# A chunked two-way RWKV scan on one core: X and Y in one product by tokens, the removal terms on the opposite half of the partitions, the state summed over 128 partitions, and the solver's transfers on GpSimd's queue

## What is computed

```python
def _rwkv_step(S, inp):
    r, w, kk, kka, kt, v = inp
    sk = jnp.einsum('bhij,bhj->bhi', S, kk)
    S = S * w[:, :, None, :] - sk[..., None] * kka[:, :, None, :] + v[..., None] * kt[:, :, None, :]
    return S, jnp.einsum('bhij,bhj->bhi', S, r)
```

## Time and profile before

| | us |
|---|---|
| three runs: lowest, median, highest | 3841.0, 3841.06, 3845.65 |
| profiled execution | 3850.02 |
| its span, first to last instruction | 3848.3 |
| PE busy / DVE / ACT / GpSimd, of the span | 3417.3 / 1747.0 / 1178.4 / 552.4 |
| mean granted TensorE clock | 0.942 of 2.4 GHz |

### The profile page before, as it was taken

The page is one execution under the profiler, slowest core; times in us unless marked ns, Lnnn a source line. Parts: engine busy times, 40 slices in busy tenths (PEclk is TensorE's granted clock), DMA queues, the critical chain, the costliest instruction groups (busy, mean ns, idle before and its releaser), DMA issues.

```text
span 3848.3 us, 65362 instructions
## 1 busy us (share of the span) xinstructions
PE 3417.3 (89%) x28861; PEld 2311.7 (60%) x28861; DVE 1747.0 (45%) x2909; ACT 1178.4 (31%) x2057; POOL 552.4 (14%) x754
## 2 busy tenths in 40 slices
PE   6999989999999898745776899898989999989998
PEld 5777776343343766545664443236757888756887
DVE  4324641121222654963356222126855546855454
ACT  3225722111111565921112111003253234334233
POOL 2220120000000210048513000001102210101210
PEclk8999998999999998867888899999999999989999
DMA  6531147989886352987533999993203313212322
GB/s 246 184 107 52 61 167 266 375 313 370 317 313 262 124 182 98 313 223 183 145 102 133 344 415 420 419 420 133 88 22 118 113 62 107 70 54 99 101 86 77
DMA packets 314859, 739.32 MB, mean 192 GB/s; under 512 B 68248, under 2 KB 148896, under 8 KB 265424
## 3 DMA queue, kind: packets, MB, share of 16 engines
q1 hardware_dynamic: 302480, 697.18, 49.7%
q0 software_dynamic: 12096, 37.96, 3.1%
HBM read 673.19 MB, written 61.89 MB: 191 GB/s over the span
## 4 chain that ended last, share of the span: by engine, by line
PE 70%; DVE 10%; DMA 8%; ACT 5%; issue 2%; SPq 2%; POOL 0%; DVEq 0%; POOLq 0%; ACTq 0%
PE ps L62 66%; DMA raw<-in_moe_w_dram 6%; PE ps L66 4%; SPq L120 2%; DVE mx L75 1%; DVE mx L102 1%; DVE mrn L99 1%; DVE b L75 1%; DVE cr L75 1%; DMA Tb<-ot 1%; DVE o L75 1%; DVE o L81 0%; ACT cr L72 0%; DMA c<-in_w_ple_gate_dram 0%; ACT lw L72 0%
## 5 line engine op out<-in xcount | busy, mean ns | idle before, releaser
L62 PE MATMUL ps<-raw,xinT 128*64 128x512 f32 (+1 forms) x4096 | 591.6, 492 | 32.8 <-DMA raw<-in_moe_w_dram 23.6
L62 PEld LDWEIGHTS ps<-raw,xinT 128*64 128x64 f32 (+1 forms) x4096 | 196.0, 123 | 401.4 <-issue 288.1
L62 PE MATMUL ps<-wp,hp 128*128 128x512 f32 x1024 | 314.1, 393 | 8.6 <-ACT wp L72 8.6
L62 PE MATMUL ps<-cr,oTr 128*128 128x512 f32 (+2 forms) x1024 | 255.6, 382 | 3.5 <-ACT oTr L72 3.1
L75 DVE TENSOR_TENSOR mx<-mx,ps 128x512 f32<-128x512 f32 (+1 forms) x196 | 127.3, 663 | 234.6 <-PE ps L62 133.3
L62 PEld LDWEIGHTS ps<-wp,hp 128*128 128x128 f32 x1024 | 193.8, 190 | 49.0 <-issue 8.8
L62 PEld LDWEIGHTS ps<-cr,oTr 128*128 128x128 f32 x1024 | 187.6, 188 | 38.9 <-ACT oTr L72 3.6
L62 PE MATMUL ps<-wp,hTr 128*128 128x512 f32 x512 | 194.4, 389 | 0.0
L62 PE MATMUL ps<-raw,hidT 128*64 128x512 f32 x768 | 177.9, 602 | 3.2 <-DMA raw<-in_moe_w_dram 3.2
L62 PE MATMUL ps<-ar,naxh 128*128 128x512 f32 x576 | 147.4, 406 | 19.0 <-DVE ar L75 8.8
L75 DVE TENSOR_TENSOR wp<-c,wp 128x1536 fp32r<-128x1536 f32 x32 | 60.6, 1894 | 180.7 <-ACT wp L72 180.7
(11 more groups left out here) (535 smaller groups left out, 6332.4 us busy)
## 6 DMA issues: line engine op xcount, KB each, us to landing
raw<-in_moe_w_dram SPq DMA_DIRECT2D x384, 1024.0 KB, 7.7
c<-in_w_in_dram SPq DMA_DIRECT2D x28, 2048.0 KB, 9.3
mx<-in_ada_w_dram SPq DMA_DIRECT2D x14, 2048.0 KB, 8.0
raw<-in_ada_w_dram SPq DMA_DIRECT2D x8, 2048.0 KB, 13.5
a<-in_na_w_qkv_dram SPq DMA_DIRECT2D x6, 2048.0 KB, 7.9
c<-in_w_branch_dram SPq DMA_DIRECT2D x16, 512.0 KB, 5.9
c<-in_w_out_dram SPq DMA_DIRECT2D x4, 2048.0 KB, 10.8
c<-in_w_ple_gate_dram SPq DMA_DIRECT2D x4, 2048.0 KB, 7.9
```

What stands on the lines that cost most here:

```text
L62: return self.e.matmul(out, lhsT, rhs, start=start, stop=stop, skip_group_check=True) if self.e is not None else self
```

## The change

- Layout of the features: far and the lent place for b and k hold, per head pair, 256 columns: r or b of chunk 0, a or k of chunk 0, a or k of chunk 1, r or b of chunk 1. So pair(c) is 128 neighbouring columns with both kinds of one chunk. load fills them in six transfers per direction (r and b in halves).
- gram: one product of 128 loaded by 128 moving columns takes the place of two of 64 by 128.
- x1 and x2 load the 128 columns of pair(c): one product gives X on one half of the partitions and the first two terms of Y, by tokens, on the other. X and U of chunk c now stand on half(1 - c). x1 and y run in two turns (one half of the heads' banks each), with a wait of PE for itself between them. The x banks are held until y has been added (y: G with U), and DVE reads Y from them after each half step.
- V and U stand in one tile VU, V on the chunk's half and U on the opposite one, and tm holds b and k likewise. So s is one product over 128 partitions that sums V's and U's part; v is gone. One bank holds both directions; DVE adds it in one operation and multiplies by the decay in two.
- load_m issues twelve transfers a round (V comes with it), load_t four. V as a whole comes no more at the start; its four latent blocks come in rows_in(2).
- The order of work in a round is new (below). x1(r, 1) stands before s, level(r + 1, 0), x1(r + 1, 0) and level(r + 1, 1) behind y.
- const, with the fence for all stores of the features, stands before the solver's first 31 rows; squares 0, 1 and 2 are read together; emm is made in two operations. GpSimd itself stores T after its squares and reads the square after next. Its product space spr is now acc's sixth block, where square 0 lies, so square 1 waits for DVE's row 30.
- Banks gives out the bank that has been unused longest, and a released one goes to the end.
- Reader takes the mean from acc in SBUF; the transposes for it are gone.

```diff
-        while self.next % 8 in self.held.values():
-            self.next += 1
-        b = self.next % 8
-        self.next += 1
+        b = next(x for x in self.queue if x not in self.held.values())
+        self.last(b)
...
+    def last(self, b):
+        self.queue.remove(b)
+        self.queue.append(b)
...
-        del self.held[key]
+        self.last(self.held.pop(key))
...
+            e.wait_ge(*P.pool.at('row', 185))
...
+            e.wait_ge(*P.dve.at('y', self.last(c), 1))
+            e.tensor_reduce(m, hv(y), AX, ADD).then_inc(*P.dve.inc())
...
+            e.tensor_tensor(hv(y), hv(y), b16(m), SUB).then_inc(*P.dve.inc())
...
+    const()
     some(31)
-    const()
...
         recur(r, 0, 'x2')
-        recur(r, 0, 'y1')
-        recur(r, 0, 'y2')
+        if more:
+            gram(r + 1, 0)
         one(r)
         recur(r, 0, 'u')
-        recur(r, 0, 'v')
-        if more:
-            gram(r + 1, 0)
-            gram(r + 1, 1)
+        recur(r, 1, 'x1')
         some(4 if r else 8)
         recur(r, 0, 's')
+        recur(r, 0, 'y')
         one(r)
-        recur(r, 0, 'y3')
-        recur(r, 1, 'x1')
         if more:
-            gram(r + 1, 2)
-            gram(r + 1, 3)
-            blocks(r + 1)
+            gram(r + 1, 1)
         some(3 if r else 8)
         one(r)
         recur(r, 1, 'x2')
-        recur(r, 1, 'y2')
         if more:
-            level(r + 1, 0)
+            gram(r + 1, 2)
+            blocks(r + 1)
         one(r)
         some(3 if r else 7)
         recur(r, 1, 'u')
-        recur(r, 1, 'v')
         if more:
-            level(r + 1, 1)
+            gram(r + 1, 3)
         recur(r, 1, 's')
-        recur(r, 1, 'y3')
+        recur(r, 1, 'y')
         some(3)
         one(r)
         if more:
+            level(r + 1, 0)
             recur(r + 1, 0, 'x1')
+            level(r + 1, 1)
         if r + 2 < 12:
             load_m(r + 2)
         if r in (2, 9):
...
+            e.wait_ge(*s_sa[n].at('sa', n))
             e.wait_ge(*P.pool.at('unit', n))
...
+    def squares(e, n):
+        for z in range(2):
+            e.dma_start(A_of(n)[64 * z:64 * z + 64], Ad[z][:, ORDER[z][n], :].rearrange("(q i) s -> q i s", i=32)).then_inc(*s_sa[n].inc())
+        s_sa[n].name('sa', n)
...
-                            out = P.psum[half(c), banks[p], i * 256 + j * 128:i * 256 + j * 128 + w * 64].rearrange("p (a n) -> p a n", a=w)
-                            ins = e.matmul(out, bk(r, z)[half(p), j, k, half(c)], ar(r, z)[half(p), 0:w, k, half(c)], (i, j) == (0, 0), True)
+                for c in range(2):
+                    cols = pair(c) if lat(r) else keys(c)
+                    for p in range(2):
+                        k = 2 * g + i
+                        ins = e.matmul(P.psum[:, banks[p], i * 256 + cols.start:i * 256 + cols.stop], bk(r, z)[half(p), k, pair(c)], ar(r, z)[half(p), k, cols],
+                                       (i, c) == (0, 0), True)
...
-                for h in range(8):
-                    for z in range(2):
-                        c = half(cut(z, i))
-                        ins = e.matmul(P.psum[c, banks[h % 2], sh(h // 2)], G(r, z)[c, h, 0:64], V[c, chunk(r, z), hd(r, h)], h < 2, False)
...
+                for turn in range(2):
+                    if turn:
+                        e.wait_ge(*P.pe.at('x1a', r, i))
+                    for k in range(4):
+                        for z in range(2):
+                            c, p = cut(z, i), z ^ turn
+                            h = 2 * k + p
+                            out = P.psum[:, banks[p], bank_of(z, k)] if lat(r) else P.psum[half(1 - c), banks[p], bank_of(z, k)]
+                            ins = e.matmul(out, G(r, z)[half(c), h, pair(c) if lat(r) else keys(c)], VU(r, z)[half(c), i, sh(h)],
+                                           k == 0 and (turn == 0 or not lat(r)), False)
+                    ins.then_inc(*P.pe.inc('x1' if turn else 'x1a', r, i))
...
+                            out = P.psum[:, banks[p], bank_of(z, k)] if lat(r) else P.psum[half(1 - c), banks[p], bank_of(z, k)]
+                            ins = e.matmul(out, ar(r, z)[half(p), k, pair(c) if lat(r) else keys(c)], state(r, z)[half(p), k, :], False, True)
                 ins.then_inc(*P.pe.inc('x', r, i))
...
-                        ins = e.matmul(P.psum[c, b, sh(h)], Z(r, z)[c, h, :], XU[c, 0, sh(h)], h == 0, True)
+                        o = half(1 - cut(z, i))
+                        ins = e.matmul(P.psum[o, b, sh(h)], Z(r, z)[o, h, :], X[o, sh(h)], h == 0, True)
...
+                    e.wait_ge(*f)
                 for z in range(2):
...
-                        e.wait_ge(*f)
-                for k in range(4):
-                    for z in range(2):
...
                         for p in range(2):
-                            c, h = half(cut(z, i)), 2 * k + p
-                            ins = e.matmul(P.psum[half(p), banks[z], sh(k)], tm(r, z)[c, 0, sh(h)], V[c, chunk(r, z), hd(r, h)], k == 0, False)
-                ins.then_inc(*P.pe.inc())
-            if what == 's' and not last:
...
-                for k in range(4):
-                    for z in range(2):
-                        for p in range(2):
-                            c, h = half(cut(z, i)), 2 * k + p
...
+                            h = 2 * k + p
+                            ins = e.matmul(P.psum[half(p), b, bank_of(z, k)], tm(r, z)[:, c, sh(h)], VU(r, z)[:, i, sh(h)], (z, k) == (0, 0), True)
                 ins.then_inc(*P.pe.inc('s', r, i))
-                for z in range(2):
...
-                            c, h = cut(z, i), 2 * k + p
-                            ins = e.matmul(P.psum[half(p), P.banks.place[('y', r, c)], sh(4 * z + k)], XU[half(c), 1, sh(h)], G(r, z)[half(c), h, 192:256],
-                                           False, True)
...
+            if what == 'y':
+                banks = [P.banks.place.get(('x', r, i, p), 0) for p in range(2)]
+                if lat(r):
+                    e.wait_ge(*P.act.at('u', r, i, 1))
+                    for turn in range(2):
+                        e.wait_ge(*(P.pe.at('ya', r, i) if turn else P.pe.at('x', r, i)))
+                        for k in range(4):
+                            for z in range(2):
+                                c, p = cut(z, i), z ^ turn
+                                h = 2 * k + p
+                                ins = e.matmul(P.psum[half(c), banks[p], bank_of(z, k)], G(r, z)[half(1 - c), h, reads(c)], VU(r, z)[half(1 - c), i, sh(h)],
+                                               False, True)
+                        ins.then_inc(*P.pe.inc('y' if turn else 'ya', r, i))
+                for p in range(2):
+                    P.banks.release(('x', r, i, p))
...
+                for z in range(2):
+                    o = half(1 - cut(z, i))
+                    for p in range(2):
+                        e.activation(X[o].rearrange("p (k e i) -> p e k i", e=2, i=64)[:, p],
+                                     P.bank('x', r, i, p)[o, 256 * z:256 * z + 256].rearrange("p (k i) -> p k i", i=64), ACT.Copy).then_inc(*P.act.inc())
...
-                elif r:
-                    e.wait_ge(*P.pe.at('recur', r - 1))
...
+                for z in range(2):
+                    o = half(1 - cut(z, i))
+                    e.activation(VU(r, z)[o, i, :], P.bank('u', r, i)[o], ACT.Copy).then_inc(*P.act.inc('u', r, i, z))
...
-            for z in range(2):
-                for j in range(11):
-                    a, b = walk[z][j], walk[z][j + 1]
-                    e.tensor_tensor(emm[:, z, :, j], Lm[:, z, :, a], Lm[:, z, :, b], ADD).then_inc(*P.dve.inc())
+            e.tensor_tensor(emm[:, :, :, 0:11], Lm[:, :, :, 0:11], Lm[:, :, :, 1:12], ADD).then_inc(*P.dve.inc())
...
+                ks = slice(4 * group(r), 4 * group(r) + 4)
+                e.tensor_tensor(St[:, :, ks, :], St[:, :, ks, :], P.bank('s', r, i).rearrange("p (z k i) -> p z k i", z=2, i=64), ADD).then_inc(*P.dve.inc('sum', r, i))
...
-                e.tensor_tensor(St[:, :, ks, :], St[:, :, ks, :], emm[:, :, ks, j:j + 1].to_broadcast([128, 2, 4, 64]), MUL).then_inc(*P.dve.inc('state', r, i))
...
+                j = 2 * step(r) + i
                 for z in range(2):
-                    seen = step(r) >= 4
+                    a = (walk[0][j] if j != 3 else 7) if z == 0 else walk[1][j + 1]
+                    e.tensor_tensor(state(r, z), state(r, z), emm[:, z, ks, a:a + 1].to_broadcast([128, 4, 64]), MUL).then_inc(*P.dve.inc())
...
-                        yo = y[:, chunk(r, z), group(r) * 512:group(r) * 512 + 512].rearrange("p (k t) -> p k t", k=4)[:, :, half(c)]
-                        src = P.bank('y', r, c)[:, 256 * z:256 * z + 256].rearrange("p (k t) -> p k t", k=4)
+                        e.wait_ge(*s_td[0].at('td', 0))
+                    for p in range(2):
```

(46 more changed lines are left out.)

205 lines of the change are left out of this document (67 added, 138 removed).

## The result

The changed kernel takes 3885.68 us (median; 3876.81 to 3890.96), the kernel before 3842.74: ratio 1.0109, 95% interval 1.0088 to 1.0129. It is 43 us slower by the medians, and 19 us less were forecast. The profiled execution has a span of 3888.9 us against 3848.3, so 40.6 us more.

The account below looks back on a forecast made before the run. Bounds seen: full DMA and DVE's rows at the start, SP's queue in rounds 0 to 3, PE's in-order stream in rounds 5 to 9. Terms: +4 -8.5 -4.3 -8.5 + 0 - 1.6 = -18.9 us; forecast 3822 us, range 3792 to 3856.

Parts of the forecast that it names:

- The change touches only the bidirectional scan and the readout behind it.: Whole kernel: only the scan's stretches and the readout were priced; nothing was forecast for the stages behind them.
- Rounds 5 to 9, -8.5: Latent rounds 5 to 9 of the scan: 25.5 for 27.2 us a round, five times, -8.5 us.
- The rival of supply: Scan rounds: SP's issues become the bound, period 24 to 32 us; at 32, +30 us, 3871; chance 0.16.
- 25.5 forecast: One latent round: PE's stream 21.4, data waits 1.9, issue gaps 1.2, half clock 1.0 us; between 23 and 28.
- more: Rival: no issue gaps or data waits (23.3 us a round), context down to 85 us; -43 us, 3798; chance 0.14.
- the rival of 36 us a round: Latent rounds: row halves don't overlap with 128 columns loaded; +75 us, 3916; chance 0.06.
- The products save records, not array time: PE in a latent round: 512 for 768 records, but 18.6 us of products, 3.7 more than before.
- Rounds 0 to 3, -8.5: Context rounds: T no longer blocked in SP's queue, levels behind y; 95 for 103.1 us, -8.5 (-25 to +5).
- Round 4, -4.3: Round 4 of the scan, which lost more to full DMA queues: 26.5 for 30.8 us, -4.3 us.
- Start, +4: From first square's transfer to first product with the state: fence now ahead of the solver, +4 us (0 to +8).
- Readout, -1.6: Readout: the mean needs no transposes, so a wait for PE and half of a reduction go, -1.6 us.
- Rounds 10 and 11, 0 (bounds -5 and +5): Last scan rounds: missing cover of Gram products costs what the shorter ACT wait returns, 0 (bounds -5 and +5).

Follow-up runs that it names:

- b_lru: The kernel before with the new bank order alone (bank unused longest, released ones to the end): 3865.35 us, ratio 1.0039.
- a_rr: The changed kernel with the old bank order, given out in turn, all else as changed: 3885.64 us, ratio 1.0096.
- turn_merge: The changed kernel with T's load first, w_o and V read behind round 5, banks in turn in the merges alone: 3820.47 us, ratio 0.9929.
- a_tf: The changed kernel with load_t(r + 1) issued ahead of load(r + 2) in each round: 3850.72 us, ratio 1.0007.
- before_rep: The kernel before with T's load first, w_o's half read behind round 5, new bank order everywhere but in the merges: 3834.59 us, ratio 0.9956.
- before_few: The kernel before with the new bank order and without the products y1 and v (640 for 768 records a latent round): 3829.41 us, ratio 0.9933.
- g_alone: The kernel before with GpSimd storing T of its squares and reading the square after next on its own queue: 3850.61 us, ratio 1.0001.
- a_const: The changed kernel with const, the fence and the loads of main and own back behind the solver's first 31 rows: 3885.38 us, ratio 1.0085.
- m1_behind: Changed kernel, T's load first, w_o and V behind round 5, banks in turn in merges alone, plus load_m(1) behind load_t(0): 3818.78 us, ratio 0.9918.
- w_behind_t: Changed kernel, T's load first, banks in turn in merges alone, load_m(1) behind load_t(0), w_o and V behind round 6's load_t and load: 3815.94 us, 0.9927.
- lru_scan_tf: The changed kernel with T's load first and the new bank order in the scan alone, banks in turn elsewhere: 3841.29 us, ratio 0.9974.

## Why the prediction was wrong

- **"The change touches only the bidirectional scan and the readout behind it."** Wrong, and so is "The change touches only the RWKV mixer" ahead of the prediction. All behind the readout stood in the forecast at nothing and measured +21.9 us. Banks is one class for the whole program, and the prediction read its new order for the scan alone. In a merge step four banks are held and four others are taken and read in between; in turn, the next step gets the four whose content DVE reads first. Oldest-first, with released banks at the end, the queue then reads branch 0, merge 0, branch 1, merge 1, and the next step's first product takes branch 0's bank, which DVE multiplies out of only behind its four additions out of the merge banks. That the order costs this time is shown by b_lru, a_rr and turn_merge.
- **Rounds 5 to 9, -8.5.** They took +8.0; of the priced terms this is the largest miss, 16.5 us. The rival of supply (SP's issues as the bound) was priced at a period of up to 32 us with a chance of 0.16, and it is what happened: 28.8 us a round. The step that failed is "against: DMA share 0.53": the share says nothing of a queue of small issues with the urgent one at its end. The issues were counted (12, 12 and 4; 15 to 23 us), and T's load behind them was the chain in the rival; it was not carried into the forecast. Moving one line (a_tf) took the round to 22.3 us. The half clock behind each wait, left out by "gaps over 1 us are gone", costs 6 us more in the half rounds behind it (16.4 for 10.3).
- **The latent round without that: 25.5 forecast, 22.3 measured.** PE's array time was sized well: 21.4 forecast, 20.8 by the starts in the trace (x2 1.8, x1 2.2, y 1.4, s and u 1.1, each twice, Gram 4.2 in all, levels 1.4), turns and shape changes in it. The terms on top were too large: waits 1.9, measured 0.8; issue gaps 1.2, measured none; half clock 1.0, and the mean clock was 0.97. The rival "more" was the nearer one, and by the prediction's own terms a round without issue gaps and data waits is 25.5 - 1.2 - 1.9 = 22.4 us, not the 23.3 that it states. Row halves do overlap with 128 columns loaded; the rival of 36 us a round is dead. "The products save records, not array time" is true of the array, but it took records for worthless. The runs show that the old round was bound by the number of PE's instructions: 768 records took 27.2, 27.0 and 27.7 us (before, b_lru, before_rep), 640 took 22.8, 35 to 36 ns each, though PE was busy only 20.1 (b_lru) and 16.1 us (before_few) of each round. From before to b_lru the waits for DVE in the five rounds fell from 19.5 to 0.7 us, and the pauses for issue rose from 17.1 to 32.5: the time stayed (136.0 and 134.9). 512 records would need 18 us by that rate and are no longer the bound. The 3.4 us for issue in the earlier trace rows were that bound, of which 1.2 was kept.
- **Rounds 0 to 3, -8.5.** Two parts fell. GpSimd's queue alone brought 2.6 of the 3 us that were forecast for it at round 2, and nothing at the end (g_alone). And SP's greater number of issues, put at 13 against 15 to 23 us, stood ahead of T at rounds 2 and 4, with V's 2 MB now behind round 2. The Trainium skill (DMA: Bandwidth & Descriptors, Issuing engines are not separate DMA queues) says that issuing from several engines saves only the sequencer's time; g_alone agrees, 1.0 us of difference between its median and that of before, and the blocked queue that was set against the rule was worth 2.6 us at round 2 and nothing at round 4.
- **Round 4, -4.3:** -6.5, right in kind. **Start, +4:** +3.5, by another cause and so by luck (a_const, m1_behind). **Readout, -1.6:** -0.5.
- **Rounds 10 and 11, 0 (bounds -5 and +5):** +7.7. Both kernels wait there for ACT (6.1 us at the longest before; 5.3 after, behind the readout's Square); the changed one runs them at a mean clock of 0.72 for 0.89 and has more array time. Moving the Square did not help. The late T does not explain them: a_tf, without it, takes 59.7 us for the same stretch, turn_merge 57.6. How the 7.7 us divide was not settled.

## What to carry to other kernels

Before costing a change to a helper that hands out banks or buffers, list every stage that calls it, and go through the order that each of them gets. In an in-order queue ask for each load how many issues stand ahead of it, and put the one that is needed first at the front: one line was worth 35 to 40 us. Where PE has pauses within a group of products without a wait, count its instructions, and the instructions from pause to pause: where the count repeats, merging products pays by their number, even when the array is no less busy.

## What the runs showed of the hardware

- In the old rounds TensorE's instructions came no faster than one MATMUL record, with its LDWEIGHTS, in 35 ns over a round, though a burst ran at 16 ns (32 records in 0.51 us). 768 records took 27.0 us and 640 took 22.8. Pauses of up to 3.2 us came in the middle of groups, 20 to 27 in five rounds, about 128 MATMUL records apart or a multiple of that (b_lru, before_few, before_rep).
- Such pauses appeared in the changed kernel as well: 3.7 us in two with 4 MB issued in round 6 (w_behind_t), but also 2.3 us in three with no such transfer in those rounds (lru_scan_tf), and none in a_tf or m1_behind. That transfers delay the supply of instructions is not shown by these runs.
- A wait of PE of 4.08 us was followed by 16.4 us at a granted clock of 0.53, most of it at 1.2 GHz (x2 3.68 us for 1.9 to 2.1), a pause of 1.78 us by 12 us at 0.58, one of 1.93 us by 20 us at 0.56 to 0.60 (w_behind_t). With nine waits of 0.5 us the five rounds ran at 0.97 (a_tf).
- Most issues of small transfers on SP took 0.5 to 0.6 us, and one up to 4.9 us behind 4 MB (1788.24); behind 4 MB the four issues of T took 10.7 us in m1_behind, where they took 2.6 to 3.2 us in rounds 5 to 9 of a_tf:

```profile
1843.13 10.70 SPq L120 DMA_DIRECT2D mx<-Td  x4
```
